# Gathering expert rows in blocks: eight u gathers, then eight v gathers

## What is computed

```python
def block(xb):                       # 128 tokens
    ...                              # router: scores, two top-16, their 256 sums, top-16 -> eidx, sc
    g = jax.nn.softmax(sc, axis=-1)
    u = peer_u[eidx]                                        # (128, 8, 16, 1024)
    a = jax.nn.gelu(jnp.einsum('nhkd,nd->nhk', u, xb))      # one dot product per token and expert
    coef = g * a
    return jnp.einsum('nhk,nhkd->nd', coef, peer_v[eidx])   # weighted sum of v rows
```

## Time and profile before

| | |
|---|---|
| median of 3 runs | 4741.9 us (4709.28 to 4750.41) |
| span of the profiled execution | 4716.2 us |
| experts stage, first to last gather issue | 1488 to 4695 us |
| gathers | 1,088 u and 1,088 v |
| busy share of the span | PE 79%, DVE 49%, ACT 16%, POOL 54% |
| idle of VectorE before its dots, all but little of it for u transfers | 1244.6 us |
| idle of TensorE before its v matmuls, most for v transfers | 778.9 us |

### The profile page before, as it was taken

How to read it: one execution, slowest core, us unless ns; L and a number is a source line. 1 busy time by engine, 2 the same in 40 slices (tenths; PEclk the granted TensorE clock), 3 DMA queues, 4 the chain that set the end, 5 groups by cost and what they waited for, 6 DMA issues and landing times.

```text
span 4716.2 us, 43591 instructions
## 1 busy us (share of the span) xinstructions
PE 3709.9 (79%) x12312; PEld 1968.6 (42%) x12312; DVE 2317.0 (49%) x5293; ACT 755.1 (16%) x1716; POOL 2539.1 (54%) x2407
## 2 busy tenths in 40 slices
PE   7999988999963887688678669668768767866777
PEld 6878764555543343243234225224324323422222
DVE  3111104443416855745745655664575574565443
ACT  3111103333320111111011101001111111110111
POOL 0000000000003777777777777777777777777776
PEclk9999988999987999999999999999999999999999
DMA  4222133332334999999999999999999999999998
GB/s 163 80 99 82 61 113 143 126 120 102 103 129 152 341 366 373 343 381 358 350 354 383 349 347 384 348 333 380 354 341 396 368 344 361 364 354 356 378 380 325
DMA packets 391889, 1318.59 MB, mean 280 GB/s; under 512 B 59552, under 2 KB 62688, under 8 KB 390592
## 3 DMA queue, kind: packets, MB, share of 16 engines
q0 software_dynamic: 326976, 1190.93, 67.6%
q1 hardware_dynamic: 64704, 125.24, 7.7%
HBM read 1261.61 MB, written 54.39 MB: 279 GB/s over the span
## 4 chain that ended last, share of the span: by engine, by line
DMA 20%; POOL 20%; PE 15%; issue 12%; DVE 2%; POOLq 0%; ACT 0%; SPq 0%; DVEq 0%
DMA vr<-in_peer_v,idx_v 15%; PE pair L1575 11%; POOL ur L1259 10%; POOL vr L1259 9%; PE pair L1548 4%; DMA ur<-in_peer_u,idx_u 3%; DMA r_hT<-h2T_d 2%; DVE ur L1493 0%; PE pair L1592 0%; DMA wpq<-in_w_pq 0%; DVE sc L1383 0%; PE pair L1559 0%; POOLq L130 0%; POOL idx_u L1283 0%; DVE besti L1389 0%
## 5 line engine op out<-in xcount | busy, mean ns | idle before, releaser
L1575 PE MATMUL pair<-vr,diag 128*128 128x512 f32 x4352 | 2140.6, 625 | 778.9 <-DMA vr<-in_peer_v,idx_v 726.6
L1493 DVE CUSTOM_DVE_ANT_0 ur<-ur,h 128x1024 f32<-128x1024 f32 x1088 | 1320.1, 1227 | 1244.6 <-DMA ur<-in_peer_u,idx_u 1167.9
L1575 PEld LDWEIGHTS pair<-vr,diag 128*128 128x128 f32 x4352 | 781.8, 195 | 2110.0 <-issue 1863.4
L1259 POOL DMA_INDIRECT ur<-in_peer_u,idx_u x1088 | 1228.2, 1129 | 369.0 <-issue 269.9
L1259 POOL DMA_INDIRECT vr<-in_peer_v,idx_v x1088 | 1206.2, 1109 | 338.7 <-issue 270.9
L1354 ACT ACTIVATE ge<-ge 128x16 f32<-128x16 f32 x68 | 14.7, 215 | 2694.2 <-DVE ge L1510 2694.2
L399 PE MATMUL pair<-w_hi,h_hi 128*128 128x512 f32 (+1 forms) x936 | 366.5, 392 | 0.7 <-issue 0.6
L399 PE MATMUL pair<-w_lo,h_hi 128*128 128x512 f32 (+1 forms) x936 | 365.7, 391 | 0.0
L399 PE MATMUL pair<-w_hi,h_lo 128*128 128x512 f32 (+1 forms) x936 | 365.3, 390 | 0.0
L1362 ACT ACTIVATE diag<-cst,coef 128x128 f32<-128x128 f32 x1088 | 325.3, 387 | 68.7 <-DVE coef L1521 58.7
L1548 PEld LDWEIGHTS pair<-r_hT,wpq 128*128 128x128 f32 x2304 | 263.8, 193 | 27.2 <-issue 25.1
(11 more groups left out here) (184 smaller groups left out, 2401.8 us busy)
## 6 DMA issues: line engine op xcount, KB each, us to landing
w<-in_w_in POOLq DMA_DIRECT2D x13, 2048.0 KB, 9.1
proj<-out_sb SPq DMA_DIRECT2D x104, 256.0 KB, 2.0
ur<-in_peer_u,idx_u POOLq DMA_INDIRECT x1088, 6.2
vr<-in_peer_v,idx_v POOLq DMA_INDIRECT x1088, 6.3
V<-proj POOLq DMA_DIRECT2D x36, 256.0 KB, 3.0
gates<-proj SPq DMA_DIRECT2D x8, 1024.0 KB, 5.0
wpq<-in_w_pq SPq DMA_DIRECT2D x4, 2048.0 KB, 15.5
KT<-skT_d SPq DMA_DIRECT2D x28, 256.0 KB, 2.7
```

The costliest lines, as they stand in the source:

```text
L1259: pool.indirect_dma_start(ring[:, k % RING, :], None, table, bass.IndirectOffsetOnAxis(ap=idx[:, k:k + 1], axis=0))\
L1493: dve.tensor_tensor_reduce(ur[r, k % RING, :], ur[r, k % RING, :], h2[r, :], 1.0, 0.0, ALU.mult, ALU.add, dots[r, parity, k:k + 1])\
L1575: last = pe.matmul(acc[:, c], diag[:, k, :], vr[:, k % RING, c], start=False, stop=True, skip_group_check=True)
```

## The change

Step by step the same gathers, holds and copies are issued by GpSimd. Their order within a step changes: u0 to u7, v0 to v7, u8 to u15, v8 to v15, in place of u0, v0, u1, v1 and so on. The first step, which has no v, is as before, and so are the 16 v gathers after the last step. No other engine's program is touched.

```diff
-                    for k in range(TOPK):
-                        if not (first(g) and k < RING):
-                            hold(pool, s["u_used"], g * TOPK + k + 1 - RING)
-                        gather(ur, peer_u[0], idx_u[:, parity], k, u_in)
+                    for half in range(TOPK // RING):
+                        ks = range(half * RING, (half + 1) * RING)
+                        for k in ks:
+                            if not (first(g) and k < RING):
+                                hold(pool, s["u_used"], g * TOPK + k + 1 - RING)
+                            gather(ur, peer_u[0], idx_u[:, parity], k, u_in)
                         if not first(g):
-                            gather_v(g - 1, 1 - parity, k)
+                            for k in ks:
+                                gather_v(g - 1, 1 - parity, k)
```

## The result

| | median | runs |
|---|---|---|
| before | 4731.6 us | 4709.3 to 4750.4 |
| after | 4529.9 us | 4527.4 to 4539.5 |

The ratio is 0.957, 95 % interval 0.953 to 0.962: the blocks make the kernel 4.3 % faster. The profiled execution has a span of 4525.8 us, 190 less than before, where the forecast had 136 less. The median was forecast at 4605 us; it lies inside A's own range.

A forecast was written before the change was run, and what follows sets the result against it. GpSimd's issue of gathers, some held up by VectorE's dots, was taken as the bound. Savings of 129 (dots) + 21 (copies) - 10 - 4 (TensorE) = 136 us from 4742 gave 4606, predicted as 4605; range 4450 to 4790.

The forecast's parts named there:

- A: Forecast case, experts stage: dots cost 0.13 to 0.26 us each, median 4605 us, range 4450 to 4681; chance 0.66.
- The bound: Experts stage: GpSimd never rests, needing 47.2 us a step for its 32 gathers; VectorE and TensorE wait for data.
- The cause: Gathers starting under a VectorE instruction with two large SBUF inputs wait for its end: 372 us, 322 of them under dots.
- the stage's first step: The one place with a pure u block: 2.15 us lost over 11 dots, 0.19 a dot, taken for the blocks.
- the bound called best: Collisions in a block: the first gather waits 0.5 us, the other seven 0.07; 1.0 a block, 0.13 a dot.
- the hiding of the router: VectorE: router parts, longest 11.2 us, fall in some 12 us without dots and end before the next u block lands.
- The copies: GpSimd's two index copies a step fall from 0.367 and 0.343 us to 0.20: 21 us saved, bounds 0 and 21.
- TensorE's price: Cost of TensorE in blocks: 10 us for half steps where its cover fails, about 4 us at the end.
- The slow start of a block: TensorE after idleness: about two v at 3.46 us instead of 1.73, so eight v take 17.4 us, not 13.9.
- Rival D: TensorE stays at 1.2 GHz through a block, eight v take 27.7 us: 740 us more, about 5480; chance 0.06.
- the tail: Stage's end on TensorE: 24 v at 1.73 us rather than 16 after v8 of the last step but one lands: about 4 us.
- Rival C: Late blocks' dots run without a pause, every second blocks GpSimd: 300 us more, 5035; decides from three blocks in ten; chance 0.10.

## Why the prediction was right

**The bound was named rightly.** GpSimd's rows add up to the stretch in both kernels, and taking its waits away twice, by other means and without the blocks, brought 300 us.

**The cause was named rightly, its size per dot was not.** Gathers that start under a dot lost 313 us in the stretch of before and 136 in that of after (each gather of the timelines sorted by what VectorE ran at its start): 0.31 and 0.13 us a dot. The prediction had 0.31 for before and took 0.19 for after, from the stage's first step. It came out at the bound called best, in part by chance: by step (two blocks) the loss under dots ranged from 0.1 to 6.5 us, with a median of 2.0. The first step is no good model: there dots started 1.23 to 2.65 us apart, so gathers met them anew several times. In the block shown above the dots settle at 1.22 to 1.24 us and one gather waits. The dots saved 177 us in the 64 steps, where the sum had 129 for all 67: 48 of the 54 us by which it fell short.

The range of A, too, was not fully worked out: no row gives its 0.26 a dot, and blocks wholly clear of gathers would by the prediction's own terms save 332 + 7 = 339 us, not 290. The result lies 80 us or more from both ends of the range.

**The step, not the hiding of the router, made most of it.** The last tile has no router work for a next tile. Seven of its steps, before (4314 to 4627 us) and after (4142 to 4435 us):

```profile
L1259 POOL DMA_INDIRECT vr<-in_peer_v,idx_v x112 | 125.1, 1117 | 34.2 <-issue 18.6 <-PE pair L1575 15.6
L1259 POOL DMA_INDIRECT ur<-in_peer_u,idx_u x112 | 113.3, 1012 | 35.7 <-issue 32.0 <-POOL idx_v L1273 3.7
```
```profile
L1259 POOL DMA_INDIRECT ur<-in_peer_u,idx_u x112 | 110.4, 986 | 35.7 <-issue 32.0 <-POOL idx_v L1273 3.7
L1259 POOL DMA_INDIRECT vr<-in_peer_v,idx_v x112 | 109.0, 973 | 34.2 <-issue 31.1 <-PE pair L1578 3.0
```

Over 0.94 us each, 238.4 - 210.6 = 27.8 us before and 219.4 - 210.6 = 8.8 after: 2.7 us a step saved without any router, of 3.0 on average over all tiles. In turn it is v that meets the dots (1117 against 1012 ns); in blocks neither.

**The copies** brought 10 us and not 21: in the stretch of after, eight still started under a dot and three under a router instruction.

**TensorE's price was about 4 us, not 14.** The slow start of a block is there as worked out, 16.84 us for eight v after 5.58 us of idleness (17.4 forecast), 14.00 after a short one. The granted clock (columns as in the earlier trace rows) was 0.50 in the first 4 us of the slow one and 1.00 from 8 us on:

```profile
2506.68 16.84 PE L1578 MATMUL pair<-vr,diag 128*128 128x512 f32 x32 [5.58 <-DMA vr<-in_peer_v,idx_v]
2526.88 14.00 PE L1578 MATMUL pair<-vr,diag 128*128 128x512 f32 x32 [1.58 <-DMA vr<-in_peer_v,idx_v]
...
2506.70:2510.70 4.00, 4.00 (x5) 1.82 (x6) 3.71 (x24) 0.00 (x0) 3.08 (x4) 0.50 1.03 423
2515.00:2523.50 8.50, 8.50 (x22) 3.76 (x21) 6.49 (x11) 0.00 (x0) 6.40 (x7) 1.00 1.03 416
```

In the 64 steps the ring hid it: GpSimd's idle time stayed what it was (664.8 us, before 664.0), so the 10 us for them did not come. Rival D fell: the lower granted clock cost nothing there. The 4 us for the tail did come. TensorE ended with 24 v in one piece, where it had 16, and GpSimd's idle time before the last 16 v gathers rose by 4.5 us (before, from 4673.4 us; then after, from 4478.9 us, and TensorE's last row):

```profile
L1259 POOL DMA_INDIRECT vr<-in_peer_v,idx_v x16 | 15.4, 964 | 6.9 <-issue 4.4 <-PE pair L1575 2.2 <-POOL idx_v L1297 0.3
...
L1259 POOL DMA_INDIRECT vr<-in_peer_v,idx_v x16 | 15.0, 938 | 11.4 <-PE pair L1578 8.5 <-issue 2.6 <-POOL idx_v L1300 0.3
4474.25 43.54 PE L1578 MATMUL pair<-vr,diag 128*128 128x512 f32 x96 [4.78 <-DMA vr<-in_peer_v,idx_v]
```

With 6 us that gathers lost less under other VectorE instructions, 48 + 10 + 6 - 11 (the copies) = 53 us make up the shortfall of 54.

**Rival C came true in two of 128 groups of eight dots.** The prediction saw less than 1 us to spare behind the longest router part. That was nearly always enough: of seven tiles, only tile 4 had head 6's first block without a pause (five of seven dots 1.15 us behind the one before), and tile 1 in part (two). It is far from the three in ten at which C decides.

## What to carry to other kernels

Where GpSimd issues indirect gathers without rest, look at the gathers' durations beside VectorE's timeline before blaming the transfers: a busy share of 0.97 for the DMA engines went with an issue-bound stage here. VectorE instructions with two large SBUF inputs are best put where GpSimd does not start anything, or stripped of one input by a copy in PSUM, which here beat the ordering. Before such an instruction is moved out of the gathers' way, see what else of GpSimd's lies where it will stand: here it moved from gathers to index copies, and nothing was gained.

## What the runs showed of the hardware

A gather waits only at its start. Held until a two-input VectorE instruction ends, it was done about 0.8 us after that instruction's row ends, even with the next one running (1.28 us from 2519.00, 2.95 us from 2286.28), where 0.94 us is its time alone. A dot that begins 0.12 us after a gather is not delayed (1.22 us). GpSimd's small copy is held up as well: 1.89 us in place of 0.20. The same dot with one input in PSUM costs 1.221 us in place of 1.226 and holds no gather up (0.97 us on average in place of 1.12). With that, in blocks, gathers of 524 KB went out every 1.24 us where nothing held them, and stretches of 700 to 1,000 us moved 402 to 405 GB/s.
